# A decoder step with expert retrieval on one core: diagonals built by ScalarE, integer route indices, a fused running maximum and a shorter gelu

## The chip, the cores and the metric

The kernel is one program on one core of a Trainium2 chip. The metric is the device time of one execution in microseconds. The kernel before takes 3795.91 us, the median of 3 runs (3793.19 to 3797.08).

## The reference, cut to what matters

One layer for 1024 prompt tokens and 64 sample tokens (8 sequences of 8): a mixer, latent attention and PEER, the expert retrieval. Attention of the sample tokens runs over 8 x 32 pages of a cache with a running maximum; PEER finds 16 experts for each of 8 heads of each token and weighs their rows of `peer_v` by a gelu of the dot with their rows of `peer_u`.

```
def page_step(carry, phys):                     # online softmax over the pages
    m_new = jnp.maximum(m, jnp.max(s, axis=-1))
    corr = jnp.exp(m - m_new)
    pr = jnp.exp(s - m_new[..., None])
    acc_new = acc * corr[..., None] + einsum(pr, c)

s_top, i_top = lax.top_k(s, 16)                 # s: (tokens, 8 heads, 2 halves, 128 keys)
cand = s_top[:, :, 0, :, None] + s_top[:, :, 1, None, :]
cand_id = i_top[:, :, 0, :, None] * 128 + i_top[:, :, 1, None, :]
best, pos = lax.top_k(cand, 16);  expert = take_along_axis(cand_id, pos);  gate = softmax(best)
a = gelu(einsum('td,ted->te', xk, peer_u[expert]))      # 128 rows of 1024 words a token
out = einsum('te,ted->td', gate * a, peer_v[expert])
```

All is float32; the two tables of experts are read by rows of 4 KB.

## The kernel before, in words

The expert work is cut into 1088 slots. A slot is one column of 128 expert numbers: GpSimd issues an indirect DMA that brings 128 rows of `peer_u` (`gather`, L1820) into a ring of 8 tiles, and, 20 slots behind (`LAG`), one that brings 128 rows of `peer_v` into a ring of 11. VectorE multiplies the u tile by the replicated tokens and sums it (`dot`, L1933), in place, which frees the ring's tile. A partition holds one (token, route) pair; four streams of 32 tokens lie beside each other.

16 slots make a unit, 68 in all. Behind the last dot of a unit `gelu_in` (L1942 to L1948) forms x + 0.044715 x^3 on VectorE for its 16 columns, ScalarE takes the tanh (L1916), and two slots later `diagonals` (L1956, L1963) forms the weights (1 + tanh) times gate times x/2, and spreads them: 16 matrices of 128x32, each a stack of four 32x32 identities times one column of weights. TensorE multiplies each by its tile of v rows (L1891) into a PSUM accumulator; that sums over the partitions and frees the v tile. The buffer for diagonals holds three units (`DIAGS`).

`Route` finds the experts of one head of 128 tokens, once a unit: top sixteen of two times 128 scores, the 256 sums, their top sixteen with positions (`pairs`, L1721 to L1731), and the decoding of the positions into expert numbers (`experts`, L1737 to L1752) by a comparison with 0 to 15, a multiplication and a sum.

Everything else, the two later groups of prompt tiles, then the pages (`Pages`), then the rest of the sample tokens (`Sample`), is laid between the slots: each engine has its program of slots as a generator, and `main.to(slot)` runs it up to that slot before the piece of other work is issued. The order on each engine is thus fixed when the program is built; each engine walks through the slots in order and waits on semaphores. `Pages` works through 64 groups of four pages (every eighth with a fifth, the new tokens), 7 slots a group: TensorE transposes a page (L2120), ScalarE copies it (`copy_page`, L2216), TensorE forms keys (L2134) and scores, ScalarE squares the keys (L2229), VectorE sums the squares (`key_norm`, L2290), ScalarE takes the root (L2240), VectorE divides, takes the maximum over the four pages (L2317), TensorE transposes that, `new_maximum` (L2322 to L2327) reduces it, joins it with the running maximum, and writes it on a diagonal and negated; ScalarE forms the correction (L2244) and the exponentials (L2249).

## Time and profile before

| | |
|---|---|
| runs | 3793.19, 3795.91, 3797.08 us |
| span of the profiled execution, first to last instruction | 3792.2 us |
| median of the runs less that span | 3.7 us |
| TensorE, VectorE, ScalarE, GpSimd busy | 2995.8, 2673.4, 954.4, 2417.9 us |
| gathers, 2 x 1088 of 512 KB each | 1140.99 of 1387.36 MB moved |

The profile is of one execution; the page gives its span and not its whole time, so the profiled execution is taken to lie 3.7 us above its span, as the median does. PE is TensorE, DVE is VectorE, ACT is ScalarE, POOL is GpSimd. The stages in time: up to about 450 us the first prompt group, mostly without gathers; to about 1850 us the second and third group between the slots; 1850 to 3200 us the pages; then the rest of the sample tokens and slots alone. Waits are read as "engine and line, waited for engine and line". "Issue" is time in which the engine waited for nothing that the profile shows.

### The profile page before, as it was taken

How to read it: one execution, taken by the hardware profiler on the slowest of the kernel's cores; microseconds unless marked ns; L12 is line 12 of the kernel's file. 1: busy time of each engine (PE TensorE's matmuls, PEld its weight loads, DVE VectorE, ACT ScalarE, POOL GpSimd, SP SyncE). 2: the span in 40 equal slices, each digit the busy share in tenths (PEclk: the TensorE clock that was granted, in tenths of full speed). 3: DMA queues.
4: the chain of work that ended last, by engine and by line, in shares of the span. 5: the costliest groups of instructions: out<-in, count | busy, mean ns of one | idle time of the engine just before them, and what ended most of it. 6: DMA issues, size and time to landing. Idle time of an engine off the chain costs nothing.

```text
span 3792.2 us, 45054 instructions
## 1 busy us (share of the span) xinstructions
PE 2995.8 (79%) x13427; PEld 1568.6 (41%) x13427; DVE 2673.4 (70%) x6884; ACT 954.4 (25%) x1899; POOL 2417.9 (64%) x2196
## 2 busy tenths in 40 slices
PE   8998878986797889987688888888888886566345
PEld 5775335533342554443344444444444443423001
DVE  2426887664578876665688988889888987554753
ACT  1211222200123320210245344434453434000100
POOL 0004556764675777665777777777777877666776
PEclk9998978998997889998799999899999998776668
DMA  6456999999999999999999999999999999999999
GB/s 223 109 196 245 334 315 366 412 409 379 368 388 354 382 373 412 409 412 367 382 374 396 390 367 387 373 398 375 385 392 393 375 393 398 413 412 407 409 391 371
DMA packets 434388, 1387.36 MB, mean 366 GB/s; under 512 B 60954, under 2 KB 119291, under 8 KB 429731
## 3 DMA queue, kind: packets, MB, share of 16 engines
q0 software_dynamic: 313344, 1140.99, 77.4%
q1 hardware_dynamic: 120802, 243.49, 18.1%
q8 instruction: 110, 1.80, 0.2%
q14 instruction: 132, 1.07, 0.1%
HBM read 1354.17 MB, written 30.11 MB: 365 GB/s over the span
## 4 chain that ended last, share of the span: by engine, by line
PE 26%; DVE 25%; DMA 20%; POOL 12%; issue 8%; DVEq 4%; ACT 2%; SPq 1%; ACTq 0%; POOLq 0%
POOL arena L1820 12%; DMA arena<-in_peer_v,arena 9%; DVE arena L1933 8%; DMA arena<-in_peer_u,arena 6%; PE ps L1891 5%; PE ps L863 4%; PE ps L2134 3%; PE ps L1196 3%; DVE arena L2290 2%; DMA arena<-in_w_peer 2%; PE ps L813 1%; PE ps L1034 1%; DMA arena<-s_dram 1%; ACT arena L1905 1%; PE ps L1011 1%
## 5 line engine op out<-in xcount | busy, mean ns | idle before, releaser
L1820 POOL DMA_INDIRECT arena<-in_peer_u,arena x1088 | 1215.7, 1117 | 828.7 <-PE ps L1174 300.3
L1933 DVE CUSTOM_DVE_ANT_0 arena<-arena 128x1024 f32<-128x1024 f32 x1088 | 1317.2, 1222 | 444.7 <-DMA arena<-in_peer_u,arena 419.3
L1820 POOL DMA_INDIRECT arena<-in_peer_v,arena x1088 | 1200.7, 1104 | 507.6 <-issue 301.5
L1891 PE MATMUL ps<-arena 128*32 128x512 f32 x4352 | 663.2, 697 | 345.7 <-DMA arena<-in_peer_v,arena 338.8
L2134 PE MATMUL ps<-arena 128*128 128x512 f32 x1056 | 544.6, 640 | 14.9 <-ACT arena L2229 12.9
L1891 PEld LDWEIGHTS ps<-arena 128*32 128x32 f32 x4352 | 141.5, 121 | 713.1 <-issue 706.5
L1196 PE MATMUL ps<-arena 128*128 128x384 f32 (+2 forms) x896 | 250.9, 433 | 53.2 <-DMA arena<-in_w_peer 53.1
L2229 ACT ACTIVATE arena<-ps 128x512 f32<-128x512 f32 x264 | 157.8, 598 | 445.4 <-PE ps L2134 426.8
L2134 PEld LDWEIGHTS ps<-arena 128*128 128x128 f32 x1056 | 191.3, 202 | 177.8 <-issue 167.7
L2142 PEld LDWEIGHTS ps<-arena 128*128 128x128 f32 x1056 | 167.0, 199 | 139.3 <-issue 137.6
L2290 DVE TENSOR_REDUCE arena<-arena 128x8 f32<-128x512 f32 x264 | 180.3, 683 | 49.3 <-ACT arena L2229 37.4
L1196 PEld LDWEIGHTS ps<-arena 128*128 128x128 f32 x896 | 154.8, 199 | 135.7 <-issue 81.1
L2165 PE MATMUL ps<-arena 128*64 128x257 f32 x528 | 140.3, 413 | 65.1 <-ACT arena L2249 65.1
L863 PE MATMUL ps<-arena 128*128 128x384 f32 (+1 forms) x528 | 172.1, 486 | 23.8 <-DVE arena L1452 23.8
L1103 PE MATMUL ps<-arena 128*128 128x384 f32 x512 | 171.5, 489 | 0.0
L2216 ACT ACTIVATE arena<-ps 128x256 f32<-128x256 f32 (+1 forms) x264 | 107.4, 407 | 247.5 <-PE ps L2120 196.8
L2142 PE MATMUL ps<-arena 128*128 128x64 f32 x1056 | 151.9, 268 | 0.0
L1905 ACT ACTIVATE arena<-arena 32x1024 f32<-32x1024 f32 x120 | 126.4, 1053 | 76.5 <-DVE arena L1933 68.3
L863 PEld LDWEIGHTS ps<-arena 128*128 128x128 f32 x528 | 103.5, 198 | 93.3 <-issue 36.9
L2120 PE MATMUL ps<-const,arena 128*128 128x128 f32 x528 | 114.0, 299 | 22.8 <-ACTq L2219 14.9
L1103 PEld LDWEIGHTS ps<-arena 128*128 128x128 f32 x512 | 96.0, 190 | 77.7 <-issue 14.1
L2165 PEld LDWEIGHTS ps<-arena 128*64 128x64 f32 x528 | 71.4, 145 | 117.3 <-ACT arena L2249 77.9
(239 smaller groups left out, 3774.7 us busy)
## 6 DMA issues: line engine op xcount, KB each, us to landing
arena<-in_w_peer SPq DMA_DIRECT2D x64, 576.0 KB, 7.8
arena<-in_w_merge SPq DMA_DIRECT2D x24, 1536.0 KB, 9.5
arena<-in_cache SPq DMA_DIRECT2D x256, 144.0 KB
arena<-in_peer_u,arena POOLq DMA_INDIRECT x1088, 8.5
arena<-in_peer_v,arena POOLq DMA_INDIRECT x1088, 8.7
arena<-in_w_front SPq DMA_DIRECT2D x33, 512.0 KB, 6.7
arena<-in_w_out SPq DMA_DIRECT2D x24, 512.0 KB, 8.9
arena<-s_dram SPq DMA_DIRECT2D x68, 128.0 KB
```

Source lines behind the costliest of these rows:

```text
L863: last = t.matmul(bank, w[:, k, :], xnT[:, k, :], start=k == 0, stop=k == KD - 1)
L1103: last = t.matmul(ps[:, 2 + 2 * (d % 2) + a, 0:T], ring[:, a * KD + k, :], xnT[:, k, 0:T], start=k == 0, stop=k == KD - 1)
L1196: last = t.matmul(ps[:, 2 + e % 2, lo * P:hi * P], self.p_item(g, j)[:, k, :], xn2T[:, k, lo * P:hi * P], start=k == 0, stop=k == KD - 1)
L1820: self.nc.gpsimd.indirect_dma_start(out=ring[:, slot, :], out_offset=None, in_=self.I[table], in_offset=bass.IndirectOffsetOnAxis(ap=self. ...
L1891: mm = self.nc.tensor.matmul(self.acc[32 * j:32 * j + 32, n, :], self.diag[:, (q0 + j) // 16 % DIAGS, (q0 + j) % 16, :], self.v_ring[:, (q ...
L1905: last = self.nc.scalar.activation(self.xrep[jg % self.XBUF][32 * i:32 * i + 32, :], self.rows[32 * j:32 * j + 32, :], ACT.Copy)
L1933: self.nc.vector.tensor_tensor_reduce(out=u, in0=u, in1=self.xrep[jg % self.XBUF], scale=1.0, scalar=0.0, op0=ALU.mult, op1=ALU.add, accum ...
L2134: last = t.matmul(self.key, self.cTp[:, j % 2, k * P:(k + 1) * P], self.wuk[:, k, :], start=k == 0, stop=k == 1)
L2142: last = t.matmul(out, self.cTp[:, j % 2, k * P:(k + 1) * P], self.qlat[:, k, b * NS:b * NS + NS], start=j + k == 0, stop=False)
L2165: last = self.nc.tensor.matmul(self.acc_ps[0:NS, 0:KL + 1], self.scs[gi % 2][:, j, :], self.source(j, par)[:, 0:KL + 1], start=j == 0, sto ...
L2229: self.nc.scalar.activation(self.sqp[:, j % 2, :], self.key, ACT.Square).then_inc(self.ksq_done, 1)
L2290: self.nc.vector.tensor_reduce(out=self.ssn[:, j, :], in_=self.sqp[:, j % 2, :].rearrange("p (h d) -> p h d", h=H), axis=AX, op=ALU.add).t ...
```

## The change

Four edits, the order of everything else is left.

- Diagonals: VectorE keeps the weights (now `weights`, with two buffers in turn) and signals; ScalarE's program has, in slot 2 of the next unit, 16 copies of the constant stack, each scaled by one column of weights. The wait for the diagonals' buffer goes with them.
- Route: the indices of the halves and of the positions stay unsigned integers, are compared and multiplied as such, and the factor 128 comes in one fused operation at the end, which writes the integer expert number.
- Running maximum: one instruction multiplies the transposed maxima by ones, and takes the maximum over them and the old running maximum. The running maximum alternates between two places, so that the copy in `accumulate` goes; ScalarE forms the correction from both with a scale of -1.
- Gelu: (x^2 + 1/0.044715) x in one operation, with the factor moved into the tanh's scale.

```
-        v.tensor_copy(self.topf, self.topi)
         v.max(out=self.best[:, 0:8], in_=candf)
         v.drain()
-        v.tensor_scalar(self.topf[:, 0, :], self.topf[:, 0, :], float(NK), None, ALU.mult)
...
-        v.tensor_copy(self.hilof, self.hilo)
-        v.drain()
-        v.tensor_tensor(self.hit, self.hilof.rearrange("p a b -> p (a b)").unsqueeze(2).to_broadcast([P, 2 * TOPK, TOPK]),
+        v.tensor_tensor(self.hit, self.hilo.rearrange("p a b -> p (a b)").unsqueeze(2).to_broadcast([P, 2 * TOPK, TOPK]),
                         self.C["iota16"].unsqueeze(1).to_broadcast([P, 2 * TOPK, TOPK]), ALU.is_equal)
...
-        v.tensor_tensor(h4, h4, self.topf.unsqueeze(2).to_broadcast([P, 2, TOPK, TOPK]), ALU.mult)
+        v.tensor_tensor(h4, h4, self.topi.unsqueeze(2).to_broadcast([P, 2, TOPK, TOPK]), ALU.mult)
...
-        v.tensor_tensor(self.ef, self.e2[:, 0, :], self.e2[:, 1, :], ALU.add)
-        v.drain()
-        v.tensor_copy(self.ids[:, u * TOPK:(u + 1) * TOPK], self.ef)
+        v.scalar_tensor_tensor(out=self.ids[:, u * TOPK:(u + 1) * TOPK], in0=self.e2[:, 0, :], scalar=float(NK), in1=self.e2[:, 1, :],
+                               op0=ALU.mult, op1=ALU.add)
...
+            u, s = divmod(k, TOPK)
+            if s == 2 and 1 <= u <= NU // 16:
+                self.diagonals(act, u - 1)
...
-        v.tensor_scalar(self.a2, self.a2, 0.044715, 1.0, ALU.mult, ALU.add)
-        v.drain()
-        v.tensor_tensor(self.th, self.a2, a, ALU.mult)
+        v.scalar_tensor_tensor(out=self.th, in0=self.a2, scalar=1.0 / GELU_CUBE, in1=a, op0=ALU.add, op1=ALU.mult)
...
+    def weights(self, dve, c):
+        v = self.nc.vector
         v.drain()
         dve.wait_ge(self.tanh_done, c + 1)
+        need(dve, self.diag_done, c - 1)
+        v.scalar_tensor_tensor(out=self.wt[:, c % 2, :], in0=self.th, scalar=1.0, in1=self.a2, op0=ALU.add, op1=ALU.mult).then_inc(self.weights_done, 1)
+
+    def diagonals(self, act, c):
+        w = self.width(16 * c)
+        n = 16 // w
+        act.wait_ge(self.weights_done, c + 1)
         if c >= DIAGS:
...
+                act.wait_ge(self.v_used[j], self.v_count[q - w0 + j])
+        for e in range(16):
+            col = e % w * n + e // w
+            last = self.nc.scalar.activation(self.diag[:, c % DIAGS, e, :], self.C["stack"], ACT.Copy, scale=self.wt[:, c % 2, col:col + 1])
+        last.then_inc(self.diag_done, 1)
...
-        self.nc.scalar.activation(self.corr, self.m, ACT.Exp, bias=self.negm).then_inc(self.corr_done, 1)
+        self.nc.scalar.activation(self.corr, self.m[(gi + 1) % 2], ACT.Exp, bias=self.m[gi % 2], scale=-1.0).then_inc(self.corr_done, 1)
...
-        v.tensor_reduce(out=self.gmax, in_=self.maxT[gi % 2], axis=AX, op=ALU.max)
-        v.drain()
-        v.tensor_tensor(self.mnew, self.m, self.gmax, ALU.max)
-        v.drain()
-        v.tensor_scalar(self.diag, self.C["ident"][0:NS, 0:NS], self.mnew, None, ALU.mult)
-        v.tensor_scalar(self.negm, self.mnew, -1.0, None, ALU.mult)
+        mnew = self.m[(gi + 1) % 2]
+        v.tensor_tensor_reduce(out=self.held, in0=self.maxT[gi % 2], in1=self.C["ones"][0:NS, :], scale=1.0, scalar=self.m[gi % 2],
+                               op0=ALU.mult, op1=ALU.max, accum_out=mnew)
+        v.drain()
+        v.tensor_scalar(self.diag, self.C["ident"][0:NS, 0:NS], mnew, None, ALU.mult)
         v.drain().then_inc(self.m_done, 1)
...
-        v.tensor_copy(self.m, self.mnew)
```

ScalarE in the page stage, at unit 33, before. L1916 is the tanh, L2249 the exponentials of a group, L2216 the copy of a transposed page, L2240 the root with its table load.

```order
L1916 ACTIVATE arena<-arena 128x16 [waits i_act_in]
L2229 ACTIVATE arena<-ps 128x512 [waits d_ks,d_key]
L2235 ACTIVATE arena<-arena 128x128 [waits d_norm_in]
L2244 ACTIVATE arena<-arena 64x1 [waits d_m]
L2249 ACTIVATE arena<-arena 128x256 [waits d_sub]
L2216 ACTIVATE arena<-ps 128x256 [waits d_s,d_t_done]
L2218 ACTIVATE arena<-arena 128x128
L2240 ACT_TABLE_LOAD
L2240 ACTIVATE arena<-arena,const 128x32 [waits d_norm_in]
```

The same place now. L1913 is the tanh, L1969 the copies, L2222 the copy of a page, L2246 the root.

```order
L1913 ACTIVATE arena<-arena 128x16 [waits i_act_in]
L2235 ACTIVATE arena<-ps 128x512 [waits d_ks,d_key]
L2241 ACTIVATE arena<-arena 128x128 [waits d_norm_in]
L2250 ACTIVATE arena<-arena 64x1 [waits d_m]
L2255 ACTIVATE arena<-arena 128x256 [waits d_sub]
L1969 ACTIVATE arena<-const,arena 128x32 [waits i_v_used2,i_v_used1,i_v_used3,i_v_used0,i_weights]
L1969 ACTIVATE arena<-const,arena 128x32 x15
L2222 ACTIVATE arena<-ps 128x256 [waits d_s,d_t_done]
L2224 ACTIVATE arena<-arena 128x128
L2246 ACT_TABLE_LOAD
L2246 ACTIVATE arena<-arena,const 128x32 [waits d_norm_in]
```

The sixteen copies stand between the exponentials and the next group's first page, and wait for the weights and for TensorE.

VectorE at the same unit, before. L1956 forms the weights, L1963 the diagonals, L2290 sums squares, an ISA row of L1933 is a dot or the reading of its sum.

```order
L2333 TENSOR_TENSOR arena<-arena,ps 128x256 [waits d_mb]
L1933 ISA arena<-arena 128x1024 [waits i_u_in1]
L1933 ISA arena 128x1
L1956 SCALAR_TENSOR_TENSOR arena<-arena 128x16 [waits i_tanh]
L1963 TENSOR_TENSOR arena<-const,arena 128x512 [waits i_v_used2,i_v_used3,i_v_used1,i_v_used0]
L2290 TENSOR_REDUCE arena<-arena 128x8 [waits d_ksq]
L2296 TENSOR_REDUCE arena<-arena 128x4 [waits d_kr_sq]
L2298 TENSOR_TENSOR arena<-arena 128x32
```

And now, with L1955 for the weights and L2296 for the squares.

```order
L2338 TENSOR_TENSOR arena<-arena,ps 128x256 [waits d_mb]
L1933 ISA arena<-arena 128x1024 [waits i_u_in1]
L1933 ISA arena 128x1
L1955 SCALAR_TENSOR_TENSOR arena<-arena 128x16 [waits i_diag,i_tanh]
L2296 TENSOR_REDUCE arena<-arena 128x8 [waits d_ksq]
L2302 TENSOR_REDUCE arena<-arena 128x4 [waits d_kr_sq]
L2304 TENSOR_TENSOR arena<-arena 128x32
```

The multiplication over 128x512 and its waits are gone; the weights wait for the diagonals of two units ago.

VectorE's running maximum, one group, before.

```order
L2322 TENSOR_REDUCE arena<-ps 64x1 [waits d_pmT]
L2324 TENSOR_TENSOR arena<-arena 64x1
L2326 TENSOR_SCALAR arena<-const,arena 64x64
L2327 TENSOR_SCALAR arena<-arena 64x1
L2290 TENSOR_REDUCE arena<-arena 128x8 [waits d_ksq]
```

And now (L2329 is the fused instruction and the reading of its result).

```order
L2329 ISA arena<-ps,const,arena 64x128 [waits d_pmT]
L2329 ISA arena 64x1
L2332 TENSOR_SCALAR arena<-const,arena 64x64
L2296 TENSOR_REDUCE arena<-arena 128x8 [waits d_ksq]
```

Three instructions on one word a partition and the reduction become the fused one; the scaled identity stays.

## Rows read from the trace of the kernel before

**Rows 1.** The page, DMA engines busy in 40 slices, tenths

```profile
DMA  6456999999999999999999999999999999999999
```

**Rows 2.** Windows: us, PE, PEld, DVE, ACT, POOL busy, clock, DMA share, GB/s

```profile
450.00:600.00 150.00, 112.16 (x516) 59.13 (x514) 129.41 (x343) 37.47 (x90) 88.35 (x83) 0.81 0.91 318
600.00:1200.00 600.00, 507.28 (x1961) 253.94 (x1961) 384.14 (x924) 100.19 (x171) 376.39 (x344) 0.91 1.00 389
...
1850.00:3200.00 1350.00, 1130.78 (x5329) 568.01 (x5330) 1188.23 (x3199) 592.04 (x1145) 1032.01 (x897) 0.94 1.01 385
...
3400.00:3600.00 200.00, 96.77 (x507) 43.72 (x506) 116.91 (x286) 14.43 (x33) 145.46 (x138) 0.65 1.03 408
```

**Rows 3.** GpSimd's waits, 1850:3200: total us, times, longest

```profile
POOL arena L1820 <- issue: 262.1, 857, 1.0
POOL arena L1820 <- DVE arena L1933: 49.4, 31, 3.2
POOL arena L1820 <- PE ps L1891: 6.4, 9, 2.2
```

**Rows 4.** GpSimd's waits, 450 to 600 us

```profile
POOL arena L1820 <- DVE arena L1933: 25.2, 12, 3.9
```

**Rows 5.** VectorE's waits, 1850 to 3200 us

```profile
DVE arena L2290 <- ACT arena L2229: 37.4, 29, 4.6
DVE arena L2305 <- ACT arena L2240: 17.2, 9, 3.9
```

**Rows 6.** Timeline, 2236 and 2402 us: start us, length us, instruction

```profile
2236.22 0.24 DVE L1752 CAST arena<-arena 128x16 uint32<-128x16 f32 x1
2236.26 0.94 POOL L1820 DMA_INDIRECT arena<-in_peer_v,arena  x1 [0.30 <-issue]
...
2402.37 1.23 DVE L1933 CUSTOM_DVE_ANT_0 arena<-arena 128x1024 f32<-128x1024 f32 x1
2402.88 1.52 POOL L1820 DMA_INDIRECT arena<-in_peer_v,arena  x1 [0.31 <-issue]
```

**Rows 7.** VectorE's groups by line: count, busy us, mean ns, idle before

```profile
L1963 DVE TENSOR_TENSOR arena<-const,arena 128x512 f32<-128x512 f32 x68 | 47.1, 693 | 16.9 <-issue 16.5
...
L1724 DVE TENSOR_SCALAR arena<-arena 128x16 f32<-128x16 f32 x68 | 19.4, 286 | 5.5 <-issue 0.4
...
L1752 DVE CAST arena<-arena 128x16 uint32<-128x16 f32 x68 | 18.2, 268 | 5.3 <-issue 0.4
...
L2322 DVE TENSOR_REDUCE arena<-ps 64x1 f32<-64x128 f32 x64 | 17.8, 279 | 1.5
...
L1944 DVE TENSOR_SCALAR arena<-arena 128x16 f32<-128x16 f32 x68 | 11.9, 175 | 5.2
...
L2338 DVE COPY arena<-arena 64x1 f32<-64x1 f32 x64 | 8.6, 135 | 0.0
```

**Rows 8.** ScalarE's groups by line: the root over 128x32

```profile
L2240 ACT ACTIVATE arena<-arena,const 128x32 f32<-128x32 f32 x56 | 18.1, 322 | 16.9 <-DVE arena L2298 16.1
```

**Rows 9.** Timeline of ScalarE, 606 to 607 us

```profile
606.48 0.22 ACT L1916 ACTIVATE arena<-arena 128x16 f32<-128x16 f32 x1 [3.30 <-DVEq L1947]
606.60 0.56 ACT L1329 ACTIVATE arena<-ps,arena 128x384 f32<-128x384 f32 x1
```

**Rows 10.** Timeline at unit 33, 2146 to 2148 us

```profile
2146.17 0.37 ACT L2216 ACTIVATE arena<-ps 128x256 f32<-128x256 f32 x1
...
2147.12 0.17 DVE L1956 SCALAR_TENSOR_TENSOR arena<-arena 128x16 f32<-128x16 f32 x1
```

**Rows 11.** Timeline of ScalarE at unit 35, 2245 to 2251 us

```profile
2245.81 0.60 ACT L2229 ACTIVATE arena<-ps 128x512 f32<-128x512 f32 x1 [1.42 <-PE ps L2134]
2250.33 0.60 ACT L2229 ACTIVATE arena<-ps 128x512 f32<-128x512 f32 x1 [3.92 <-PE ps L2134]
```

**Rows 12.** Timeline at the last unit, 3761 to 3769 us

```profile
3761.20 0.18 DVE L1956 SCALAR_TENSOR_TENSOR arena<-arena 128x16 f32<-128x16 f32 x1
...
3767.91 1.48 PE L1891 MATMUL ps<-arena 128*32 128x512 f32 x6 [0.65 <-DMA arena<-in_peer_v,arena]
```

More of the change, by code:

```diff
@@ L34 @@
 EPS = 1e-6
+GELU_CUBE = 0.044715
 RING = 8
@@ L1791, in __init__ @@
         self.x0_in, self.xt_in, self.x_set, self.h_in = sem("i_x0_in"), sem("i_xt_in"), sem("i_x_set"), sem("i_h_in")
-        self.act_in, self.tanh_done, self.diag_done, self.collected = (sem("i_" + n) for n in ("act_in", "tanh", "diag", "collected"))
+        self.act_in, self.tanh_done, self.weights_done, self.diag_done, self.collected = (
+            sem("i_" + n) for n in ("act_in", "tanh", "weights", "diag", "collected"))
         self.stored = sem("i_stored")
@@ L1915, in scalar @@
                     act.wait_ge(self.act_in, u + 1)
-                    self.nc.scalar.activation(self.th, self.th, ACT.Tanh, scale=0.7978845608028654).then_inc(self.tanh_done, 1)
+                    self.nc.scalar.activation(self.th, self.th, ACT.Tanh, scale=0.7978845608028654 * GELU_CUBE).then_inc(self.tanh_done, 1)
+            u, s = divmod(k, TOPK)
+            if s == 2 and 1 <= u <= NU // 16:
+                self.diagonals(act, u - 1)
             t = (k + 24) // 128
@@ L1949, in gelu_in @@
                                in1=self.gates[:, col:col + TOPK * w].rearrange("p (j s) -> p j s", j=w)[:, :, s:s + n], op0=ALU.mult, op1=ALU.mult)
-    def diagonals(self, dve, c):
-        v, w = self.nc.vector, self.width(16 * c)
+    def weights(self, dve, c):
+        v = self.nc.vector
         v.drain()
         dve.wait_ge(self.tanh_done, c + 1)
-        v.scalar_tensor_tensor(out=self.wt, in0=self.th, scalar=1.0, in1=self.a2, op0=ALU.add, op1=ALU.mult)
-        v.drain()
+        need(dve, self.diag_done, c - 1)
[4 more added lines that the diff above has]
+        act.wait_ge(self.weights_done, c + 1)
         if c >= DIAGS:
@@ L1984, in vector @@
             if s == 1 and 1 <= u <= NU // 16:
-                self.diagonals(dve, u - 1)
+                self.weights(dve, u - 1)
             if k in EIGHT_AT:
@@ L2022, in __init__ @@
         small = take(NS, 8)
-        self.m, self.mnew, self.negm, self.corr, self.gmax, self.rl = (small[:, j:j + 1] for j in range(6))
+        self.m, self.corr, self.rl = [small[:, j:j + 1] for j in range(2)], small[:, 2:3], small[:, 3:4]
+        self.held = take(NS, P)
         self.diag, self.acc, self.lat = take(NS, NS), take(NS, KL + 1), take(NS, KL)
@@ L2367, in vector @@
                 if self.group(gi - 2)[3] > GP:
-                    self.divide(dve, self.group(gi - 2)[0])
+                    self.divide(dve, self.group(gi - 2)[0], gi - 1)
             for j in range(5):
```

22 lines of the change are left out of this document (9 added, 13 removed).

## The prediction

> **What bounds the kernel now.** I read four views in this order. First the 40-slice picture of DMA: from the fifth slice to the end every slice stands at 9 tenths or more, so the transfers, not one engine, fill nearly the whole run [rows 1]. Second, busy time by stage, because a mean over the span mixes stages. The reader is to see that from 600 us on the DMA share is 1.00 to 1.03, that VectorE is busy 384 of 600 us while the last prompt work runs, and 1188 of 1350 us (88%) in the page stage (1850 to 3200 us), and that one window is different: 450 to 600 us, with 318 GB/s, a DMA share of 0.91 and VectorE at 129 of 150 us [rows 2]. Third, what GpSimd waits for, since GpSimd issues both gathers of every slot. In the page stage its time closes exactly: 1032 us inside gathers, 262.1 us in the 0.3 us that follow each of them, 49.4 us waiting for VectorE's dots (a free place in the ring of eight u rows) and 6.4 us waiting for TensorE (a free v row): 1350 us [rows 2, 3]. So here GpSimd is held back by somebody else for 55.8 us only, in 40 waits; less the 0.3 us that each would have cost anyway, 44 us. That is the most that a faster VectorE can give back in this stage. Fourth, what VectorE itself waits for there: ScalarE, 37.4 us for the squares and 17.2 us for the roots [rows 5]. Nearly all else of the stage it works. So VectorE is the engine that runs behind, and GpSimd, with 96% of its time in gathers and what follows them, the one that nearly sets the pace.
>
> The DMA gives a second ceiling. In 3400 to 3600 us, where almost nothing but 4 KB rows moves, the share is 1.03 at 408 GB/s; in the page stage it is 1.01 at 385 GB/s [rows 2]. If 1.03 is what full looks like, the page stage can shrink by 2% of 1350, 26 us, before the transfers themselves stop it; the smaller packets of the pages are part of why 385 is lower than 408, so I do not use the ratio of the bandwidths.
>
> **The change part by part, on VectorE.** A unit is 16 slots, there are 68 units; about 28 fall in the page stage (1350 us at some 48 us each).
> - Diagonals: one 128x512 multiplication of 693 ns goes, and with it the gap of about 0.25 us in front of it, less the overlap with its neighbour: 0.85 us a unit [rows 7].
> - Gelu: the scale-and-add of 175 ns goes; with the drain behind it, it took the place of 0.25 us (the other operation becomes one with two steps, of the same size) [rows 7].
> - Route: the change drops two conversions and one addition of 175 to 185 ns each (the gelu row stands for these three, of the same size), one multiplication of 286 ns, and turns the last conversion of 268 ns into a fused operation that I put at the same price. The first conversion lies half under its neighbour; with two drains that leave, 0.95 us a unit [rows 7]. Comparing and multiplying integers against floats I take to cost what the float form costs; no row here shows the mixed form. The bounds are nothing and, if it were to fall to half speed, 0.69 us more for each of the two 128x512 operations (the size of the row of L1963), 1.4 us a unit.
> - Together 2.05 us a unit, 28 x 2.05 = 57 us in the page stage.
> - Running maximum: a reduction of 279 ns, two operations of about 150 ns (the copy's row of 135 stands for them) and the copy go; one fused instruction over 64x128 comes in. The kernel's one other fused product-and-reduce costs 1.23 us for 1024 elements [rows 6] and reads its accumulator in another instruction; the nearest by size is the reduction over the same 128 elements, 279 ns [rows 7]. Between these ends I take 0.4 us with the read, by the nearer; what stays (the scaled identity) costs the same as before. Saved about 0.25 us a group, 64 groups: 16 us.
>
> So VectorE loses 73 us of its 1188 in the page stage, 6%, three times what 44 us of GpSimd's waits would need if each microsecond reached them.
>
> **On ScalarE.** 16 copies of 128x32 with a scale from memory replace the multiplication. The nearest row is a square root over 128x32 with an operand from memory: 322 ns busy [rows 8]. Back to back they overlap: a 0.22 us tanh is followed 0.12 us after its start by the next instruction [rows 9]. Bounds 16 x 0.12 = 1.9 us and 16 x 0.32 = 5.2 us; I take 0.22 each, 3.5 us a unit, which is the duration of the small activation without its overlap. No table load is added, since the order shows none and copies follow roots and exponentials in the kernel already.
>
> This block is new work in the middle of an in-order queue, behind a wait for VectorE (the weights) and for TensorE (the diagonals' buffer of three units ago, long free). What is queued behind it: in the page stage the copy of a transposed page, the table load and the roots. For unit 33 the weights end at 2147.29 us and the copy of the page ran at 2146.17; now it starts near 2150.9, 4.7 us later [rows 10]. For unit 35 the queue in front ends at 2246.4, the copies fit before the next activation at 2250.33, delay nothing [rows 11]. The units repeat in a pattern of seven, between these two ends; with 2.5 us on average the block costs the page chain up to 28 x 2.5 = 70 us. How much reaches VectorE decides. At unit 33 VectorE still has two tile reductions and two dots in front of the operation that needs the root, and the root would come some 2 us late instead of 4.7. I let a third pass on, 25 us: 73 - 25 = 48 us net of VectorE's lateness, against 44 us of GpSimd's waits. Since waits don't all lie where the relief falls, half to a third of them go: 16 us, inside the DMA ceiling of 26.
>
> **TensorE's side.** The diagonals come later by the hand-over and 3.5 us less 0.7. The tightest place is the last unit: its weights ended at 3761.38 us and its first product ran at 3767.91, released by a gathered v row [rows 12]. The copies would be done at 3765, 3 us early, and with 5.2 us a block still 1 us early. So I cost the end at nothing. Its cover is the v transfer; if ScalarE's block were longer than 6.5 us, it would be the end itself.
>
> **The other stages.** In 450 to 600 us VectorE holds GpSimd for 25.2 us in 12 waits [rows 4]; three units there save 3 x 2.05 = 6 us of VectorE at 86%, I take 4 of it. From 600 to 1850 and after 3200 us the DMA share is full and the saving turns into waiting for rows: nothing. The prompt work ahead of the first unit has none of it but the first routes, under 1 us.
>
> A place where a rule and a row differ. A gather that starts while the 1.2 us dot runs takes 1.52 us instead of 0.94: it starts at 2402.88, the dot ends at 2403.60, and it ends 0.8 us behind it [rows 6]. A gather that starts 0.04 us into one of the conversions that go takes 0.94 us, undisturbed [rows 6]. So removing the conversions shortens no gather in my sum. The Trainium skill, page "SBUF — State Buffer", section "Who interferes with whom", says that copies, casts and tensor_scalar in a two-port mode lock GpSimd out of its port while an operation with two SBUF inputs disturbs only GpSimd's reads. By that rule the four operations that leave would free up to 0.9 us of lock a unit; the trace does not bear it out at these sizes.
>
> **Sum.** 3792.2 us of span - 16 - 4 = 3772; the median of the runs stands 3.7 us above the span of the profiled execution, so about 3776. I round toward no change, for what the new wait may cost in the prompt stage: 3778 us, 0.5% faster. What a measurement of this kernel can tell from no change is about 0.2%, 7.6 us.
>
> **Rivals.**
> 1. The transfers hide it. From 600 us on the DMA share is 1.00 or more; if 1.01 is full in the page stage too, VectorE's 73 us become waits for rows. For it: the share. Against it: GpSimd waits for rings in 40 places there although it is otherwise never idle, and the share reached 1.03 later. Time: 3796 - 4 = 3792, within 0.2%.
> 2. ScalarE's block sets the pace of the page chain (slower). If a copy costs 0.32 us the block is 5.2 us, the average delay 4.2 us, 118 us in the page stage, and if all of it reaches VectorE the relief of 73 is overdrawn by 45 us. It decides from a delay passed on of 73/28 = 2.6 us a unit. For it: VectorE already waits 54.6 us for exactly these ScalarE instructions [rows 5]. Against it: ScalarE is busy 592 of 1350 us [rows 2] and mostly ahead. All of it gives 3841, half of it 3818; I name 3818.
> 3. More comes back than I allow: all 44 us in the page stage, 10 us in 450 to 600 us, and 6 more where VectorE holds GpSimd between 600 and 1850 us: 3736. For it: VectorE is the engine that is late, and a ring that is never full needs only 3% more speed. Against it: the DMA ceiling of 26 us.
> 4. By the page's rule on the lock, worked out from rows: 0.95 us of route operations a unit, 68 units, each microsecond taken off a gather: 65 us at most, 3731 us. The undisturbed gather speaks against it.
>
> **Chances.** The forecast (a gain of 8 to 30 us) 0.44, rival 1 0.26, rival 2 0.15, rival 3 0.13, rival 4 0.02. Faster: the forecast nearly whole, rivals 3 and 4: 0.58. Within 0.2%: rival 1 and the forecast's edge, 0.26. Slower 0.16. The forecast's own range is 3765 to 3788; the range for 8 in 10 reaches into rivals 2 and 3: 3748 to 3808.
>
> **What would show it.** Right: in the page stage VectorE's busy time falls by about 70 us in spite of a shorter stage, GpSimd's wait for VectorE falls from 49.4 to about 30 us or less, the DMA share rises to 1.02, and ScalarE's copies stand at 0.2 us apart. Wrong: VectorE's waits for the squares and roots grow beyond 54.6 us by more than 50; 128x512 route operations longer than 0.7 us; a first product of the last unit released by ScalarE; or a page stage of the same length with more time in VectorE's wait for u rows.

## The result, and the profile after

The kernel after takes 3757.28 us (median of 4 runs, 3753.22 to 3759.55), the kernel before 3796.49 us beside it; the ratio is 0.9902 [0.9889, 0.9914]. Two later measurements of the changed kernel gave 0.9909 [0.9894, 0.9924] and 0.9924 [0.9911, 0.9937]. That is 29 to 37 us, where the forecast had 18 (0.9953). The direction and the wide range (3748 to 3808) held. The gain is about double by the first two measurements; the 3757 lies outside the forecast's own range (3765 to 3788), while the 29 us of the third would just have been inside it.

First the windows of the changed kernel, with the columns of [rows 2].

```profile
450.00:600.00 150.00, 109.67 (x542) 57.70 (x534) 127.95 (x330) 44.99 (x128) 95.03 (x84) 0.83 0.91 323
600.00:1200.00 600.00, 502.20 (x1931) 246.77 (x1930) 374.30 (x869) 138.94 (x341) 379.78 (x347) 0.91 1.00 391
1200.00:1850.00 650.00, 526.77 (x2375) 275.93 (x2375) 427.05 (x1036) 157.04 (x426) 444.47 (x418) 0.90 1.00 392
1850.00:3200.00 1350.00, 1145.67 (x5410) 577.67 (x5409) 1154.64 (x2936) 678.38 (x1582) 1055.80 (x911) 0.93 1.02 391
```

Against [rows 2], the page stage holds 911 gathers instead of 897 in the same 1350 us, VectorE is busy 34 us less and ScalarE 86 us more, and the DMA share rises from 1.01 to 1.02 with 385 to 391 GB/s (in e8 and e15, the same kernel measured again, 907 and 900 gathers with a share of 1.01). Look at 1200 to 1850 us too, which before reads

```profile
1200.00:1850.00 650.00, 524.02 (x2318) 273.36 (x2317) 440.16 (x1103) 109.87 (x208) 431.70 (x410) 0.88 1.00 388
```

Four traces of the code of before have 410 to 413 gathers there (before, e3, e11, e18), three of the changed kernel 418, 418 and 419, with the share at 1.00 to 1.01 in all. The share had not said that this stage was full. From 600 to 1200 us the three gathers more and the 391 instead of 389 GB/s show nothing: e3, whose code there is that of before, has 348 gathers and 392 GB/s.

Then the waits of GpSimd and of VectorE after, 1850 to 3200 us (total us, times, longest), which answer to [rows 3] and [rows 5]:

```profile
POOL arena L1817 <- issue: 272.1, 890, 1.0
POOL arena L1817 <- DVE arena L1933: 18.9, 11, 3.1
POOL arena L1817 <- PE ps L1888: 3.4, 10, 0.7
...
DVE arena L2296 <- ACT arena L2235: 58.4, 53, 4.8
DVE arena L2311 <- ACT arena L2246: 32.4, 16, 4.2
DVE arena L1933 <- DMA arena<-in_peer_u,arena: 14.7, 9, 5.6
```

GpSimd waits 18.9 us for dots instead of 49.4 (21.1 and 23.5 in e8 and e15). VectorE waits 90.8 us for ScalarE's squares and roots instead of 54.6, and 14.7 us for u rows: it now runs ahead of the transfers at times.

The prediction closed the balance of waits for the page stage alone. Over 600 to 1850 us GpSimd's waits for other engines are, before:

```profile
POOL arena L1820 <- PE ps L1891: 125.6, 52, 23.3
POOL arena L1820 <- DVE arena L1933: 101.1, 54, 8.6
```

and after:

```profile
POOL arena L1817 <- PE ps L1888: 124.2, 53, 23.4
POOL arena L1817 <- DVE arena L1933: 85.6, 53, 6.7
```

So from 600 to 1850 us GpSimd was held back by VectorE for 101 us, twice the 49.4 us of the page stage, and by TensorE for 126. That 15.5 us of it went can't be read from these two traces: e3, with the code of before up to the first page, has this:

```profile
POOL arena L1820 <- DVE arena L1933: 83.3, 47, 8.7
```

The new and changed instructions, from the changed kernel's groups by line (busy us, mean ns, then idle before):

```profile
L1969 ACT ACTIVATE arena<-const,arena 128x32 f32<-128x32 f32 x1088 | 237.7, 307 | 150.5 <-DVE arena L1955 150.5
L1739 DVE TENSOR_TENSOR arena<-arena,const 128x512 f32<-128x512 uint32 x68 | 47.9, 704 | 5.8 <-issue 0.9
L1743 DVE TENSOR_TENSOR arena<-arena 128x512 f32<-128x512 f32 x68 | 47.1, 692 | 5.1
L1747 DVE SCALAR_TENSOR_TENSOR arena<-arena 128x16 uint32<-128x16 f32 x68 | 11.9, 175 | 5.5 <-issue 0.4
L2332 DVE TENSOR_SCALAR arena<-const,arena 64x64 f32<-64x64 f32 x64 | 25.0, 391 | 5.2 <-issue 0.3
L2329 DVE CUSTOM_DVE_ANT_0 arena<-ps,const,arena 64x128 f32<-64x128 f32 x64 | 21.7, 340 | 2.2 <-issue 1.3
L2329 DVE DVE_READ_ACCUMULATOR2_ANT arena<- 64x1 f32 x64 | 4.8, 75 | 0.0
```

and the last unit's block on ScalarE in the timeline (start us, length us), with the first product behind it:

```profile
3720.75 3.50 ACT L1969 ACTIVATE arena<-const,arena 128x32 f32<-128x32 f32 x16 [0.36 <-DVE arena L1955]
...
3727.07 1.91 PE L1888 MATMUL ps<-arena 128*32 128x512 f32 x8 [0.64 <-DMA arena<-in_peer_v,arena]
```

The prices of the new instructions came out near their estimates: 16 copies in 3.50 us, integer comparison 704 ns, fused maximum 415 ns with its read. The last unit's products are still released by rows of v.

### The profile page after: what moved, and what is told of

The parts are those of the page before. It is cut to its first block, busy times and chain, and to the rows that moved or that the text cites. A ratio compares the mean times of both kernels' runs of the same rounds, so it can differ in the third digit from the quotient of the medians.

```text
span 3751.4 us, 45400 instructions
## 1 busy us (share of the span) xinstructions
PE 3014.1 (80%) x13427; PEld 1575.6 (42%) x13427; DVE 2575.9 (69%) x6348; ACT 1184.7 (32%) x2987; POOL 2443.3 (65%) x2196
## 3 DMA queue, kind: packets, MB, share of 16 engines
q14 instruction: 136, 1.11, 0.1%
## 4 chain that ended last, share of the span: by engine, by line
PE 27%; POOL 23%; DMA 18%; DVE 14%; issue 10%; ACT 4%; DVEq 3%; SPq 1%; ACTq 0%; POOLq 0%
POOL arena L1817 23%; DMA arena<-in_peer_v,arena 9%; PE ps L1888 5%; PE ps L864 5%; DVE arena L1933 4%; DMA arena<-in_peer_u,arena 4%; PE ps L1197 3%; PE ps L2140 3%; DMA arena<-in_w_peer 2%; PE ps L814 2%; DMA arena<-s_dram 1%; DMA s_dram<-arena 1%; ACT arena L1969 1%; ACT arena L1902 1%; PE ps L1035 1%
## 5 line engine op out<-in xcount | busy, mean ns | idle before, releaser
L1817 POOL DMA_INDIRECT arena<-in_peer_u,arena x1088 | 1214.0, 1116 | 780.2 <-issue 304.8
L1933 DVE CUSTOM_DVE_ANT_0 arena<-arena 128x1024 f32<-128x1024 f32 x1088 | 1318.7, 1222 | 487.7 <-DMA arena<-in_peer_u,arena 461.2
L1817 POOL DMA_INDIRECT arena<-in_peer_v,arena x1088 | 1227.8, 1128 | 493.7 <-issue 303.5
L1888 PE MATMUL ps<-arena 128*32 128x512 f32 x4352 | 679.7, 708 | 327.9 <-DMA arena<-in_peer_v,arena 317.4
L1969 ACT ACTIVATE arena<-const,arena 128x32 f32<-128x32 f32 x1088 | 237.7, 307 | 150.5 <-DVE arena L1955 150.5
L2140 PEld LDWEIGHTS ps<-arena 128*128 128x128 f32 x1056 | 190.6, 201 | 180.6 <-issue 173.4
L2296 DVE TENSOR_REDUCE arena<-arena 128x8 f32<-128x512 f32 x264 | 180.4, 683 | 73.4 <-ACT arena L2235 61.8
L2148 PEld LDWEIGHTS ps<-arena 128*128 128x128 f32 x1056 | 165.3, 197 | 137.2 <-issue 135.2
L1197 PEld LDWEIGHTS ps<-arena 128*128 128x128 f32 x896 | 154.2, 199 | 134.3 <-issue 77.5
L2222 ACT ACTIVATE arena<-ps 128x256 f32<-128x256 f32 (+1 forms) x264 | 107.1, 406 | 199.8 <-PE ps L2126 139.9
L864 PEld LDWEIGHTS ps<-arena 128*128 128x128 f32 x528 | 102.8, 196 | 91.7 <-issue 35.0
L1913 ACT ACTIVATE arena<-arena 128x16 f32<-128x16 f32 x68 | 14.4, 212 | 368.9 <-DVEq L1945 368.9
```

The lines of the kernel that those rows point to most:

```text
L864: last = t.matmul(bank, w[:, k, :], xnT[:, k, :], start=k == 0, stop=k == KD - 1)
L1197: last = t.matmul(ps[:, 2 + e % 2, lo * P:hi * P], self.p_item(g, j)[:, k, :], xn2T[:, k, lo * P:hi * P], start=k == 0, stop=k == KD - 1)
L1817: self.nc.gpsimd.indirect_dma_start(out=ring[:, slot, :], out_offset=None, in_=self.I[table], in_offset=bass.IndirectOffsetOnAxis(ap=self. ...
L1888: mm = self.nc.tensor.matmul(self.acc[32 * j:32 * j + 32, n, :], self.diag[:, (q0 + j) // 16 % DIAGS, (q0 + j) % 16, :], self.v_ring[:, (q ...
L1933: self.nc.vector.tensor_tensor_reduce(out=u, in0=u, in1=self.xrep[jg % self.XBUF], scale=1.0, scalar=0.0, op0=ALU.mult, op1=ALU.add, accum ...
L1969: last = self.nc.scalar.activation(self.diag[:, c % DIAGS, e, :], self.C["stack"], ACT.Copy, scale=self.wt[:, c % 2, col:col + 1])
```

## Where in the run the time went

The start of a given dot is a clock that all kernels share. Dot 78 starts at 602 us before, dot 464 opens the page stage, dot 896 closes it, 1087 is the last; dot 304 halves the way to the pages. The rows of the kernel before, then of the changed one (timelines of VectorE; start us, length us):

```profile
601.89 1.22 DVE L1933 CUSTOM_DVE_ANT_0 arena<-arena 128x1024 f32<-128x1024 f32 x1
...
1373.13 1.22 DVE L1933 CUSTOM_DVE_ANT_0 arena<-arena 128x1024 f32<-128x1024 f32 x1
...
1904.09 1.23 DVE L1933 CUSTOM_DVE_ANT_0 arena<-arena 128x1024 f32<-128x1024 f32 x1
...
3203.19 1.23 DVE L1933 CUSTOM_DVE_ANT_0 arena<-arena 128x1024 f32<-128x1024 f32 x1 [0.58 <-issue]
...
3758.84 1.23 DVE L1933 CUSTOM_DVE_ANT_0 arena<-arena 128x1024 f32<-128x1024 f32 x1 [1.33 <-DMA arena<-in_peer_u,arena]
```

```profile
587.95 1.22 DVE L1933 CUSTOM_DVE_ANT_0 arena<-arena 128x1024 f32<-128x1024 f32 x1
...
1352.18 1.22 DVE L1933 CUSTOM_DVE_ANT_0 arena<-arena 128x1024 f32<-128x1024 f32 x1
...
1876.02 1.23 DVE L1933 CUSTOM_DVE_ANT_0 arena<-arena 128x1024 f32<-128x1024 f32 x1
...
3157.68 1.22 DVE L1933 CUSTOM_DVE_ANT_0 arena<-arena 128x1024 f32<-128x1024 f32 x1 [0.49 <-issue]
...
3718.03 1.22 DVE L1933 CUSTOM_DVE_ANT_0 arena<-arena 128x1024 f32<-128x1024 f32 x1 [1.33 <-DMA arena<-in_peer_u,arena]
```

The dots of the traced kernels give this table (us). One trace is one execution, so the first column has every kernel whose code in that stretch is the one of before (that of e3 up to dot 452).

| stretch | code of before | changed kernel, three traces | no decoding (e12) | forecast |
|---|---|---|---|---|
| to dot 0 | 334.3, 334.2 (e3), 332.2 (e4), 331.8 (e18), 334.1 (e10), 329.9 (e9), 327.3 (e2) | 329.2, 325.8, 330.4 | 323.2 | -1 |
| dot 0 to 78 | 267.5, 267.8 (e3), 268.8 (e11), 267.7 (e18) | 258.8, 264.5, 264.1 | 260.4 | -4 |
| 78 to 464 | 1302.2, 1292.9 (e3), 1295.7 (e11), 1295.4 (e18) | 1288.1, 1287.9, 1287.8 | 1275.5 | 0 |
| 464 to 896, pages | 1299.1, 1298.7 (e11), 1299.2 (e17) | 1281.7, 1285.4, 1292.4 | 1281.1 | -16 |
| 896 to 1087 | 555.7, 553.7 (e3), 555.3 (e11), 560.2 (e17) | 560.4, 557.0, 557.2 | 554.3 | 0 |

By the means, -3.5, -5.5, -8.6, -12.5 and +2 us. Up to dot 78, in the page stage and at the end this is near the forecast. What is missing lies most of all between dot 78 and 464, which is 600 to 1850 us: there the forecast had nothing, all three traces of the changed kernel are quicker than all four with the code of before, and e12, with still less on VectorE, is quicker by another 12 us. Equal code differs by up to 9 us in this stretch and by 7 us ahead of dot 0. It is not so with every kernel that has the route edit: e13 and e6 take 1301.5 and 1301.3 us from dot 78 to 464, both in traces of the slowest of their six runs.

The second half of the way, dot 304 to 464, scatters less and says more. The five traces with route, gelu and the move of the diagonals (the changed kernel's three, e7 and e14) take 522.9 to 523.8 us; all fourteen that lack one of the three, or have the multiplication back (e6), take 527.7 to 531.0, and e12 519.8. The route edit alone brings 2 us there (e1, 528.0), the others alone 1 or nothing, all three together 7. Here the edits don't add up: the last of them brings 5 us.

## The experiments

All ratios are to the kernel before, run beside it on the same chip, with their 95% intervals. "Alone" means that one edit of the diff, on the kernel before.

**e1, the route edit alone.**

> The kernel before with the route edit alone (integer indices, four small VectorE instructions a unit fewer). Theory A, every stage in which VectorE is late gives time back: 0.95 to 1.05 us a unit off VectorE, so 0.5 of the whole saving, ratio 0.994 to 0.996, with the first dot about 5 us earlier since the first four routes stand in a row ahead of the first gather. Rival, the transfers are the bound and only the start counts: 0.9985, the first dot 5 us earlier and nothing after it.

Measured 0.9946 [0.9931, 0.9962], 20 us, more than the 18 us given to the whole change. In its page stage VectorE's wait for ScalarE is 61 us and GpSimd's for dots 22.2 us.

**e2, the diagonals on ScalarE alone.**

> The kernel before with the diagonals moved to ScalarE and nothing else. Theory A: 0.85 us a unit off VectorE, 0.995 to 0.997, ScalarE's block of 3.5 us costs less than a third of it. Rival, ScalarE's block passes on to VectorE: 0.999 to 1.003.

Measured 1.0011 [0.9999, 1.0023]. In its page stage, GpSimd's wait for dots and VectorE's two for ScalarE, against [rows 3] and [rows 5]:

```profile
POOL arena L1821 <- DVE arena L1937: 77.3, 44, 4.6
...
DVE arena L2301 <- ACT arena L2240: 55.3, 44, 4.4
DVE arena L2316 <- ACT arena L2251: 34.9, 18, 4.2
```

VectorE has a 0.69 us instruction less in each unit, and yet holds GpSimd up longer, 77.3 us. Its own waits for ScalarE rose from 54.6 to 90.2 us.

**e3, the running maximum alone, and e4, the gelu alone.**

> The kernel before with the running maximum alone in one instruction. Theory A: 0.25 us a group, 64 groups, at most 16 us of VectorE in the page stage, half of it shows: 0.998. Rival: it shortens the chain of a group from maximum to exponentials, which TensorE and ScalarE wait for, and gives more than VectorE's saving: 0.995.

> The kernel before with the shorter gelu alone: 0.25 us a unit, 17 us of VectorE over the run. Theory A: a third to a half of it, 0.998 to 0.9985. Rival, transfers hide it: 1.000.

Measured 0.9991 [0.998, 1.0003] and 0.9999 [0.9987, 1.0012]: each within what can be told from nothing. For the gelu that is the rival's 1.000; for the maximum neither 0.998 nor 0.995.

**e5 and e16, the changed kernel with the diagonals left on VectorE**, measured at two times.

> The changed kernel with the diagonals left on VectorE (route, maximum and gelu edits). Theory B, after the four single runs (0.9946, 1.0011, 0.9991, 0.9999): the diagonals' move is worth nothing, so this is as fast as the whole change, 0.990 to 0.992. Rival, the edits need each other (single ratios multiply to 0.9947, the whole has 0.9902): 0.9935 to 0.9945, and the move to ScalarE earns 0.3 to 0.4% once VectorE has the room.

> The changed kernel with the diagonals on VectorE as before. Both theories: 0.9925 to 0.995. If it comes within 0.001 of the changed kernel in this call, the diagonals' move is worth nothing either way, and the whole's gain is that of the route edit with little else.

Measured 0.9936 [0.9915, 0.9957] and 0.9908 [0.9893, 0.9922]. Beside e5 the whole was ahead by 0.3%, beside e16 (e15, 0.9924) behind by 0.2%. Over both, the move of the diagonals is worth nothing that these runs can tell. e16 lies outside both theories' range. The waits of e16 in the page stage:

```profile
POOL arena L1816 <- DVE arena L1929: 9.7, 4, 3.8
POOL arena L1816 <- PE ps L1887: 0.9, 3, 0.3
...
DVE arena L2285 <- ACT arena L2224: 43.9, 34, 4.6
...
DVE arena L2300 <- ACT arena L2235: 18.8, 12, 3.8
```

Without the copies VectorE's waits for ScalarE are 62.7 us instead of 90.8, and GpSimd waits 9.7 us for dots instead of 18.9.

**e6, the changed kernel with the 128x512 multiplication back on VectorE as idle work.**

```
         (weights)
+        v.drain()
+        v.tensor_tensor(rt.hit (as 4x4x32), stack, wt, ALU.mult)
```

> The changed kernel (ScalarE still makes the diagonals that are used) with a multiplication over 128x512 of the same form put back on VectorE, into a scratch tile, behind the weights. It has both costs. If VectorE's time in the later stages counts: 0.9925 to 0.9945, the difference to the whole change being the price of 0.7 us a unit on VectorE. If transfers cover it: 0.9902 as the whole.

Measured 0.993 [0.9915, 0.9946], against 0.9909 for the same kernel without it (e8, measured with it): 0.2%, 8 us for 0.69 us a unit, with intervals that overlap. GpSimd's wait for dots is 37.5 us.

**e7, the copies spread over four slots, and e8, the changed kernel again.**

```
-            if s == 2 and 1 <= u <= NU // 16:
-                self.diagonals(act, u - 1)
+            if 2 <= s <= 5 and 1 <= u <= NU // 16:
+                self.diagonals(act, u - 1, s - 2)      # four of the sixteen
```

> The changed kernel with the sixteen copies in four slots (2 to 5), four in each, and one signal at the end. If the block of 3.5 us in the middle of ScalarE's queue is what eats the gain of the diagonals (VectorE's waits for squares and roots rose from 54.6 to 90.8 us in the page stage), these waits fall by a third and the time to 0.988 to 0.989. Rival, it is ScalarE's total work: no change against 0.9902.

> The changed kernel as it is, beside the three, so that they can be compared on one chip: 0.989 to 0.9915.

Measured 0.9921 [0.9907, 0.9934] and 0.9909 [0.9894, 0.9924]. VectorE's waits for ScalarE in the page stage are 83.8 us spread, 88.7 us in one block. Cutting the block in four gains nothing; the waits fell by 5 us and not by a third.

**e9, before without the multiplication from unit 4 on, and with no copies** (the diagonals of the first units are used for all, so the weights in the output are others).

```
+        if c >= DIAGS:
+            last.then_inc(self.diag_done, 1)
+            return
```

> The kernel before without the multiplication that makes the diagonals, from the fourth unit on: the weights are formed and signalled, TensorE uses the diagonals of the first three units again, ScalarE gets nothing (the output of the experts is not the reference's). VectorE's relief of the diagonals' move, without its price on ScalarE. Theory C, any microsecond taken off VectorE is worth a third: 0.9945 to 0.9965, and ScalarE's block then costs what the move alone lost, 0.5%. Rival, the route's place in the order is special: 0.999 to 1.001.

Measured 0.9951 [0.9937, 0.9964], 19 us: what the relief half of the diagonals' edit is worth by itself.

**e10, before with 15 idle copies a unit on ScalarE**, behind the diagonals' semaphore.

```
+            if s == 2 and 1 <= u <= NU // 16:
+                act.wait_ge(self.diag_done, u)
+                for e in range(15):
+                    self.nc.scalar.activation(self.twice[:, e, :], self.C["stack"], ACT.Copy, scale=self.C["eps"])
```

> The kernel before, unchanged on VectorE, with 15 copies of 128x32 into a scratch tile on ScalarE in slot 2 of each unit, behind a wait for the unit's diagonals. The price on ScalarE without the relief. Theory C: 1.003 to 1.006, VectorE's waits for squares and roots in the page stage 85 to 95 us as in the changed kernel. Rival, ScalarE has room: 0.999 to 1.001.

Measured 1.0084 [1.007, 1.0098], 32 us slower and more than either theory allowed. The page stage, its window and then its waits:

```profile
1850.00:3200.00 1350.00, 1119.64 (x5239) 563.82 (x5240) 1167.40 (x3127) 662.15 (x1539) 980.83 (x881) 0.94 1.00 377
```
```profile
POOL arena L1821 <- DVE arena L1939: 115.7, 70, 4.0
...
DVE arena L2296 <- ACT arena L2235: 48.3, 48, 2.9
DVE arena L2311 <- ACT arena L2246: 31.7, 17, 4.2
```

GpSimd's wait grew from 49.4 to 115.7 us although VectorE's waits for ScalarE grew only from 54.6 to 80.0. Dot 464 starts at 1904.2 us, as before, dot 896 at 3234.4 instead of 3203.2: all of the loss is in the page stage. What the block does is to be seen at one unit, in ScalarE's timeline:

```profile
2152.41 0.42 ACT L2255 ACTIVATE arena<-arena 128x256 f32<-128x256 f32 x1 [1.43 <-DVE arena L2339]
2154.82 3.29 ACT L1922 ACTIVATE arena<-const 128x32 f32<-128x32 f32 x15 [1.99 <-DVE arena L1969]
2158.02 0.36 ACT L2222 ACTIVATE arena<-ps 128x256 f32<-128x256 f32 x1
```

ScalarE stands idle for 1.99 us for VectorE's diagonals, works 3.29 us on the copies, and only then copies the page that was transposed in the meantime.

**e11, the route edit in the four units ahead of the first gather only.**

> The kernel before with the route edit in its first four units alone, those that run ahead of the first gather. If the earlier start (first dot 3 to 8 us earlier in the traces) comes from them: 0.9985 to 0.9993. The kernels with no edit there had the first dot up to 7 us earlier too, so the rival is that it is scatter: 0.9998 to 1.0002.

Measured 0.999 [0.9981, 0.9999], 4 us with an interval that ends at nothing; its first dot starts at 329.8 us.

**e12, the changed kernel without the decoding** (comparison, multiplication and sum dropped; the expert numbers are position times 63 plus an index, so other rows are fetched and the output is another).

```
-        (the eight lines of the decoding)
+        v.scalar_tensor_tensor(out=self.ids[...], in0=self.pos, scalar=63.0, in1=self.topi[:, 0, :], op0=ALU.mult, op1=ALU.add)
```

> The changed kernel with the decoding of the positions left out (two small, three 128x512 operations; the expert number is 63 times the position plus the first index, so other rows are fetched than the reference's). Another 2.3 us a unit off VectorE. It asks how far a lighter VectorE still goes. If the transfers' ceiling is near: 0.987 to 0.990. If VectorE still sets the pace at a third a microsecond: 0.975 to 0.978.

Measured 0.9826 [0.9812, 0.9839]. Another 2.3 us of VectorE a unit (the busy time falls from 2575.9 to 2423.2 us, 2.2 us a unit) bring another 0.8%, between the two forecasts: some 31 us for 153, a fifth a microsecond. By the table the most of it, 20 us against the changed kernel's means, comes ahead of the pages; the page stage, 1281.1 us, is no shorter than the changed kernel's best.

```profile
1850.00:3200.00 1350.00, 1136.89 (x5433) 569.30 (x5433) 1085.20 (x2765) 676.93 (x1590) 1055.62 (x914) 0.93 1.02 394
```

VectorE is down to 1085 us there and GpSimd makes 914 gathers to the changed kernel's 911. VectorE's waits for ScalarE's squares and roots are up to 114.6 us:

```profile
DVE arena L2284 <- ACT arena L2223: 61.6, 53, 4.6
DVE arena L2299 <- ACT arena L2234: 53.0, 25, 4.6
```

**e13, route and diagonals; e14, the whole without the maximum; e15, the whole.** Measured together, with e16.

> Before with the route edit and the diagonals on ScalarE, without the maximum's and gelu's. Theory A (the two edits lean on each other: the copies cost ScalarE time that is worth less once VectorE's route work is short): 0.9915 to 0.993, below the product of the single ratios. Theory B (edits add up, the whole's further gain is scatter or lies in maximum and gelu beside the copies): 0.9946 times 1.0011, 0.9957, within 0.001.

> The changed kernel with the running maximum of before (route, diagonals and gelu changed). Theory A: 0.991 to 0.9925, as the maximum alone gave 0.9991. Theory B (the maximum is what lets the copies pay, as it shortens the chain behind ScalarE's block in the page stage): 0.9955 or more, and VectorE's waits for ScalarE above 95 us in the page stage.

> The changed kernel, for the same chip and runs of before as its neighbours. Both theories: 0.9890 to 0.9920. Above 0.993 would say that the further gain over the three edits without the diagonals is scatter.

Measured 0.9943 [0.9926, 0.9959], 0.9937 [0.9924, 0.995] and 0.9924 [0.9911, 0.9937]. None of the three lies in a range named for it. Route with the diagonals is the route alone; gelu and maximum then add 0.06% and 0.13%, neither clear of nothing. The theory that the route edit alone lets the copies pay has no support left. The traces hint at the other one: from dot 464 to 896 they take 1302.4 us (e13) and 1299.2 (e14), no less than before, and 1292.4 with the maximum (e15). The ratio of e14 speaks against a large part of it, and VectorE's waits for ScalarE are 90.3 us there and not above 95.

**e17, the route edit in the 34 units decoded ahead of the page stage, and e18, in the 34 from it on.**

```
+                rt.experts(dve, EXPERTS_AT[k], EXPERTS_AT[k] < 34)      # e18: >= 34
```

> Before with the route edit in the first 34 of the 68 units, which are decoded ahead of the page stage. The prediction's step (from 600 to 1850 us nothing, 450 to 600 us some 4 us, the first routes under 1 us): 0.998 to 1.000, and the dots of the page stage 5 us earlier at its end as at its start. The theory formed since (each microsecond off VectorE is worth a third wherever gathers run): half of the route edit's 0.9946, 0.996 to 0.998.

> Before with the route edit in the last 34 units, 28 of them in the page stage. The prediction's step: nearly all of the route edit's gain, 0.994 to 0.996. The theory formed since: the other half, 0.9965 to 0.9985.

Measured 0.9976 [0.9966, 0.9987] and 0.997 [0.9959, 0.9981]; their product, 0.9946, is e1. The theory formed since held in both. The first half alone brings 9 us, where the forecast had about 2 (its 5 us ahead of the pages for the whole change, times the route's share of the relief, 0.95 of 2.05). That would be 0.9994, outside the interval; the range that was named, 0.998 to 1.000, the interval still touches. The second half brings 11 us, less than the 15 to 23 of the step. But e17 alone does not place its gain in 600 to 1850 us: about 4 of its 9 us are those of e11, whose four units it includes, and its trace has 259.0 us from dot 0 to 78 (268.0 with the code of before), and from dot 78 to 464 1291.8, only 1 us under the lowest with the code of before. Its dot 464 starts 23 us earlier than in the one trace of before, more than the ratio allows, and dot 896 by no more than that.

```profile
1880.94 1.23 DVE L1947 CUSTOM_DVE_ANT_0 arena<-arena 128x1024 f32<-128x1024 f32 x1
...
3180.18 1.22 DVE L1947 CUSTOM_DVE_ANT_0 arena<-arena 128x1024 f32<-128x1024 f32 x1 [0.23 <-issue]
```

The trace of e18 doesn't show its own 11 us where they should be: it takes 1298.2 us from dot 464 to 896, as before. For e18 the ratio stands and the place is not shown.

## Why the prediction was wrong, step by step

- "From 600 to 1850 and after 3200 us the DMA share is full and the saving turns into waiting for rows: nothing." This is the step that failed, for its first half. About 9 us came there (dot 78 to 464: 1287.9 us against 1292.9 to 1302.2), and 21 us with the decoding gone (e12, 1275.5). The share of 1.00 was read as a ceiling, while GpSimd's 101.1 us of waits for dots in that window stood in no balance. Which wait made room is not shown, since these waits scatter in equal code from 83 to 101 us. After 3200 us, with a share of 1.02 to 1.03 up to 3600 us, "nothing" held, in e12 too.
- 450 to 600 us, 4 us: 5.5 by dot 0 to 78, of which 4.1 from dot 37 (450 us) on. Right.
- "The first routes, under 1 us": 4 us by e11, and 3.5 by the start of the first dot. Both are less than what the traces scatter by there, 7 us.
- The page stage, 16 us: 12.5 by the mean of three traces (7 to 17). Right in size and in two of its signs (GpSimd's wait 18.9 us, share 1.02). The ceiling that was set at 26 us showed itself at 18: in e12 the stage gets no shorter, with a share of 1.02.
- VectorE's relief: overrated, and its sign missed. The busy time was to fall by about 70 us in the page stage. It fell by 34 in the window and by 42 for equal work (1145.1 to 1103.0 us from dot 464 to 896). With the gaps, take VectorE's own time: a stretch less VectorE's waits for other engines and for rows. From dot 464 to 896, 27 units, it is 1246.2, 1246.2 and 1246.6 us with the code of before (before, e11, e17) and 1188.6 to 1189.0 in the changed kernel: 57 us went and not 71. By edits: route 0.86 us a unit instead of 0.95 (e1), the diagonals 0.76 (e2) to 0.92 (e9) for 0.85, gelu 0.31 for 0.25, the maximum 0.11 us a group for 0.25 (e3). The maximum's durations give 0.21 (279 + 153 + 300 + 150 + 135 before, 340 + 75 + 391 after), since the scaled identity became 91 ns longer; part of the rest must have overlapped its neighbours. So the right size of the page stage is in part luck: less relief than forecast, more of it paid.
- What relief brings: of the route's 50 us of own time between the first dot and the last, 20 us arrived, 0.4 us for each, and by halves 9 and 11 us, about the same rate. In e9 it is 19 of 59, 0.3, and in the whole change 29 to 37 of 125. In the page stage the rest comes back as waits for ScalarE and for rows: e1 has 23 us less own time, 16 us more waits and a stage 7 us shorter, e9 25, 14 and 11. In the sum only the copies lengthened such waits.
- ScalarE's block: its length, 3.5 us, was exact, and 25 us passed on to VectorE in the page stage were 28 (90.8 us of waits, against 62.7 in e16) to 36. What was wrong is its price. In e10 all waits of VectorE from dot 464 to 896 rise by 28 us with its own time within 3 us of before, and the stretch by 31: they are paid in full, while 1 us of relief brings 0.3 to 0.4. In the forecast both had one price, so the diagonals' edit counted as a net gain; it gives -19 us (e9) and +23 (e2 less e9) to +32 (e10). Over e2, e13 and the pairs with e5 and e16 that is nothing that these runs can tell. Rival 2's mechanism is real, at the size of the relief that pays for it. Why added waits are paid in full and relief is not, is not shown; that VectorE and GpSimd take turns at setting the pace would do it, and is a guess. e7 says that the block's being in one piece isn't it.
- Rival 1 (the transfers hide it) falls for the pages and the prompt, and holds after 3200 us. Rival 4 falls: the mean gather of u rows is 1116 ns after and 1117 before, that of v rows 1128 and 1104. By the Trainium skill, "SBUF — State Buffer", "Who interferes with whom", the conversions that went should have freed GpSimd; no trace here has it, at 16 or 32 words a partition: in the page stage of before 45 gathers start inside a conversion or a tensor_scalar, and take 0.93 to 0.95 us.
- Rival 3 (3736, more comes back) had the right idea for 600 to 1850 us, with 6 us where 9 came, and too much for the page stage.
- The profiled executions stand 1.8 to 1.9 us above their spans (3753.22 to 3751.4 in the changed kernel), not 3.7; if that holds for the kernel before, its profiled execution was 2 us quicker than its median.

So of the 11 to 19 us between the forecast and the measurements, 9 lie between dot 78 and 464 and some 4 ahead of it, by the table, while the pages and the end give 5 back; the rest the traces don't place. The single edits multiply to 0.9947, the whole was 0.9902, 0.9909 and 0.9924, 9 to 17 us better. Of that, 4 us are found between dot 304 and 464, where the edits pay only together; the rest stays open, and the same kernel differed by 0.28% between two measurements (e5, e16). Of edits worth less than that, these runs can't tell the sign.

No version tried beats the changed kernel beyond doubt. The one without the move of the diagonals is as fast (0.9908, 0.9936), with 230 us less work on ScalarE.

## What to carry to other kernels

Close the balance of waits of the pacing engine for every stage before a stage is written off. A DMA share of 1.00 is no ceiling while the issuing engine still waits for somebody: from 1200 to 1850 us 410 to 413 gathers became 418 or 419, and 422 in e12, with the share unmoved. Take several traces of equal code before a wait or a stretch is said to have changed. And don't trade work between two engines at one price per microsecond: put into the in-order queue of an engine that others wait for, 3.5 us cost as much as 0.7 us with its gap saved elsewhere.

## What the runs showed that was not expected

- GpSimd's time in gathers rises when its waits fall. In the page stage 897 gathers take 1032.01 us before (1.15 us each), 881 take 980.83 in e10 (1.11), and in e16 903 take 1066.21 (1.18): 

```profile
1850.00:3200.00 1350.00, 1139.74 (x5410) 570.99 (x5408) 1169.03 (x2950) 586.46 (x1131) 1066.21 (x903) 0.93 1.01 390
```

  A gather that starts beside a dot takes 1.4 us in the mean (379 of the 897 of before; 1.52 in [rows 6]), and one that doesn't wait meets a dot somewhat more often (398 of 903 in e16, 334 of 881 in e10). Of the 45 us of waits that e16 takes away in this stage (9.7 and 0.9 us left of the 55.8 of [rows 3]), 34 went into the gathers, six more of them and longer ones; 8 of these 34 are one gather of 8.7 us. This is one way in which a freed microsecond is lost, and it was missing in the sum.
- The decoding lengthens gathers too. Of gathers that meet no dot, those that start inside the comparison or the multiplication over 128x512 take 1.06 us in the mean before (53 in the whole run) and 1.27 us in the changed kernel (71, at most 1.46), against 0.94 us for those that start inside the sum over the same 128x512. The order is the same and the two operations are as long as before, so what makes it 1.27 us isn't shown; it costs GpSimd some 17 us, of the 25 by which its busy time rises (2417.9 to 2443.3 us).
- The scaled identity of 64x64 takes 391 ns (381 in e3) instead of 300 when its scalar comes from the accumulator of the fused operation just before it.
- A comparison of 128x512 unsigned integers with floats takes 704 ns, that of floats 692; the multiplication of floats by unsigned indices 692, by floats 717.
- Copies of 128x32 with a scale from memory follow each other 0.213 us apart (15 steps in 3.50 less 0.31 us), each 307 ns long.
- Executions of the same code differ by up to 9 us over 1565 us of gathers (dot 0 to 464, 1569.8 before and 1560.7 in e3), so a trace alone doesn't place 10 us.
